# Gate and up tiles of a SwiGLU layer: three products into 256 columns in place of two into 512 and 256, and no sums of halves

## The reference, cut to what matters

```python
    ffn = (jax.nn.silu(h @ w_ffn_gate[l]) * (h @ w_ffn_up[l])) @ w_ffn_down[l]
    h = layer_norm(DEEPNORM_ALPHA * h + ffn, ln2_g[l], ln2_b[l])
```

## Time and profile before

| | |
|---|---|
| median of 3 runs | 1360.66 us |
| lowest and highest | 1360.02 and 1361.16 us |
| the profiled execution, from its first to its last instruction (span) | 1358.1 us |
| TensorE matmuls busy | 1348.0 us, 99% |
| TensorE weight loads busy | 1213.2 us, 89% |
| VectorE busy | 890.4 us, 66% |
| ScalarE busy | 651.7 us, 48% |
| mean granted TensorE clock | 0.999 of full speed |

### The profile page before, as it was taken

The page is one execution under the profiler, slowest core; times in us unless marked ns, Lnnn a source line. Parts: engine busy times, 40 slices in busy tenths (PEclk is TensorE's granted clock), DMA queues, the critical chain, the costliest instruction groups (busy, mean ns, idle before and its releaser), DMA issues.

```text
span 1358.1 us, 25677 instructions
## 1 busy us (share of the span) xinstructions
PE 1348.0 (99%) x9644; PEld 1213.2 (89%) x9644; DVE 890.4 (66%) x1320; ACT 651.7 (48%) x910; POOL 23.0 (2%) x50
## 2 busy tenths in 40 slices
PE   9999999999999999999999999999999999999998
PEld 8999999999999998878888888888888888888897
DVE  6787868677785766578666666666666655545545
ACT  5556556474656444355444444444444453334332
POOL 0022000000000000000000000000000000000000
PEclk9999999999999999999999999999999999999999
DMA  8656544445465776644656555555555665556563
GB/s 282 202 190 182 163 150 155 156 145 167 141 183 184 242 228 199 230 173 136 195 184 196 186 187 192 191 187 190 191 189 186 208 231 192 189 171 201 170 204 106
DMA packets 79773, 253.19 MB, mean 186 GB/s; under 512 B 16544, under 2 KB 17504, under 8 KB 79584
## 3 DMA queue, kind: packets, MB, share of 16 engines
q1 hardware_dynamic: 78304, 251.69, 56.5%
q0 software_dynamic: 1408, 0.63, 0.2%
HBM read 248.08 MB, written 2.10 MB: 184 GB/s over the span
## 4 chain that ended last, share of the span: by engine, by line
PE 98%; DVE 1%; ACT 1%; DMA 0%; issue 0%; SPq 0%; DVEq 0%
PE ps L890 23%; PE ps L893 12%; PE ps L879 11%; PE ps L880 10%; PE ps L881 10%; PE ps L902 9%; PE ps L904 9%; PE ps L903 9%; PE ps L1098 1%; PE ps L1117 1%; PE ps L1094 1%; DMA xrow<-x 0%; PE ps L1029 0%; PE ps L1070 0%; PE ps L1043 0%; PE ps L1051 0%
## 5 line engine op out<-in xcount | busy, mean ns | idle before, releaser
L464 DVE TENSOR_TENSOR wlo<-raw,whi 128x1024 fp32r<-128x1024 f32 x450 | 546.6, 1223 | 287.1 <-ACT whi L508 286.0
L508 ACT ACTIVATE whi<-raw 128x1024 fp32r<-128x1024 f32 x450 | 475.1, 1057 | 406.6 <-PE ps L904 184.8
L890 PE MATMUL ps<-hT,whi 128*128 128x512 f32 x1376 | 477.1, 390 | 0.0
L893 PE MATMUL ps<-hT,wlo 128*128 128x256 f32 x1376 | 388.0, 282 | 0.0
L890 PEld LDWEIGHTS ps<-hT,whi 128*128 128x128 f32 x1376 | 258.3, 188 | 54.1
L893 PEld LDWEIGHTS ps<-hT,wlo 128*128 128x128 f32 x1376 | 260.1, 189 | 0.0
L879 PE MATMUL ps<-xT,whi 128*128 128x256 f32 x784 | 224.1, 286 | 0.6 <-DVE wlo L464 0.6
L880 PE MATMUL ps<-xT,whi 128*128 128x256 f32 x784 | 219.0, 279 | 0.0
L881 PE MATMUL ps<-xT,wlo 128*128 128x256 f32 x784 | 218.6, 279 | 0.0
L879 PEld LDWEIGHTS ps<-xT,whi 128*128 128x128 f32 x784 | 147.4, 188 | 1.9 <-issue 1.1
L880 PEld LDWEIGHTS ps<-xT,whi 128*128 128x128 f32 x784 | 147.5, 188 | 0.2
(11 more groups left out here) (271 smaller groups left out, 1407.0 us busy)
## 6 DMA issues: line engine op xcount, KB each, us to landing
raw<-slabs SPq DMA_DIRECT2D x450, 512.0 KB, 3.8
xrow<-x SPq DMA_DIRECT2D x4, 512.0 KB, 6.8
rows<-x SPq DMA_DIRECT2D x4, 512.0 KB, 6.7
gb<-ln_rows SPq DMA_DIRECT2D x4, 512.0 KB, 7.9
eraw<-slabs SPq DMA_DIRECT2D x4, 512.0 KB, 7.0
gb<-ln_rows SPq DMA_DIRECT2D x1, 2048.0 KB, 8.3
out<-rows SPq DMA_DIRECT2D x8, 256.0 KB, 2.4
yb<-u SPq DMA_DIRECT2D x32, 24.0 KB, 3.1
```

The costliest lines, as they stand in the source:

```text
L464: unit.tensor_tensor(wlo[:, s, :], raw[:, s, :], whi[:, s, :].bitcast(F32), ALU.subtract).then_inc(done, 1 + empty_after)
L508: nc.scalar.activation(whi[:, s, :], raw[:, s, :], ACT.Copy).then_inc(hi_ready, 1 + empty + first)
L890: mm(ps[:, bank, :], hi, src[:, kt].rearrange("p a t -> p (a t)"), start=(first and n == 0), stop=False)
L893: ins = mm(ps[:, bank, TOK:512], lo, src[:, kt, 0, :], start=False, stop=done)
```

## The change

The gate and up tiles are made by `fold_tile`, and `feature_tile` goes. The sums of halves (L1872, 88 of them) go, with `tmp[0]` and `tmp[2]`: the Silu reads bank 0 (bank 4 in the second pair) itself, and the product reads bank 1 (bank 5) itself. What frees a bank is now the Silu for the gate's and the product for the up's (`ffn_silu`, `ffn_prod`), so these two semaphores take the place of `row_free` in this stage, and the counts of `row_free` behind it become smaller by 88. VectorE makes its third low part before it waits for the up tile, and its fourth after the product and not before it. All buffers stay at their addresses.

```diff
@@ ScalarE
-                    ac.wait_ge(row_free, i * 4 + 11 + 2 * e)
-                    nc.scalar.activation(tmp[:, 1, :], tmp[:, 0, :], ACT.Silu).then_inc(ffn_silu, 1)
+                    if first and e == 0:
+                        ac.wait_ge(early_used, 1)
+                    else:
+                        ac.wait_ge(slab_used, i * FFN_PER + (FFN0 + 4 * e + 2))
+                    nc.scalar.activation(tmp[:, 1, :], ps[:, 4 if first and e == 1 else 0, 0:TOK], ACT.Silu).then_inc(ffn_silu, 1)
...
@@ TensorE
-            def feature_tile(bank, s, b, src, kts, first, last, whi=whi, wlo=wlo):
-
-                for n, kt in enumerate(kts):
-                    hi = whi[:, s, (b + n) * P:(b + n + 1) * P]
-                    lo = wlo[:, s, (b + n) * P:(b + n + 1) * P]
-                    mm(ps[:, bank, :], hi, src[:, kt].rearrange("p a t -> p (a t)"),
-                       start=(first and n == 0), stop=False)
-                    done = last and n == len(kts) - 1
-                    ins = mm(ps[:, bank, TOK:512], lo, src[:, kt, 0, :], start=False, stop=done)
-                return ins
...
-            def panel(src, src_ready, n_slabs, slot0, v, low, m):
+            def panel(src, src_ready, n_slabs, slot0, v, low, m, read=()):
...
                     if k == 0:
                         row_bank(m + t)
+                        if read:
+                            pe.wait_ge(read[t], FT)
...
-                    ins = feature_tile(e, 2 * e + h, n, hT, (k,), k == 0, k == KT - 1, ehi, elo)
+                    ins = fold_tile(e, 2 * e + h, n, hT, (k,), k == 0, k == KT - 1, ehi, elo)
...
                     if not bank:
-                        row_bank(i * 4 + (8 + e))
+                        pe.wait_ge((ffn_silu, ffn_prod)[e % 2], i * 2 + e // 2)
                     for h in range(2):
                         k = 2 * e + h
                         late_low(i * FFN_PER + (FFN0 + k))
-                        feature_tile(bank + e % 2, k % RING, 0, hT, range(8 * h, 8 * h + 8), h == 0, h == 1
-                                     ).then_inc(slab_used, 1)
+                        fold_tile(bank + e % 2, k % RING, 0, hT, range(8 * h, 8 * h + 8), h == 0, h == 1
+                                  ).then_inc(slab_used, 1)
...
@@ VectorE
-                    lows(0, 1)
-                    tile_sum(tmp[:, 0, :], 0, v + 1)
-                    lows(2)
-                    tile_sum(tmp[:, 2, :], 1, v + 3)
+                    lows(0, 1, 2)
+                    if first and e == 0:
+                        ve.wait_ge(early_used, 2)
+                    else:
+                        ve.wait_ge(slab_used, v + 4)
+                    ve.wait_ge(ffn_silu, n + 1)
+                    V.tensor_tensor(tmp[:, 3, :], tmp[:, 1, :], ps[:, 5 if first and e == 1 else 1, 0:TOK], ALU.mult
+                                    ).then_inc(ffn_prod, 1)
                     lows(3)
-                    ve.wait_ge(row_free, i * 4 + (12 + 2 * e))
-                    ve.wait_ge(ffn_silu, n + 1)
-                    V.tensor_tensor(tmp[:, 3, :], tmp[:, 1, :], tmp[:, 2, :], ALU.mult).then_inc(ffn_prod, 1)
```

More of the change, by code:

```diff
@@ L872, in row_bank, with fold_tile @@
                 pe.wait_ge(row_free, m + 1)
-            def fold_tile(bank, s, b, src, kts, first, last):
+            def fold_tile(bank, s, b, src, kts, first, last, whi=whi, wlo=wlo):
                 for n, kt in enumerate(kts):
@@ L1273, in _ @@
                     panel(act, act_lo, DOWN_PER, DOWN_PER * p, i * (2 * DOWN_PER) + DOWN0 + DOWN_PER * p, late_low,
-                          i * 4 + (8 + 2 * FT + 2 * p))
-            panel(act, act_lo, DOWN_PER, 2 * DOWN_PER, DOWN0 + 2 * DOWN_PER, late_low, 8 + 2 * FT + 4)
-            v, m = DOWN0 + 3 * DOWN_PER, 8 + 2 * FT + 6
+                          i * 4 + (8 + 2 * p), (ffn_silu, ffn_prod) if p == 0 else ())
+            panel(act, act_lo, DOWN_PER, 2 * DOWN_PER, DOWN0 + 2 * DOWN_PER, late_low, 8 + 4)
+            v, m = DOWN0 + 3 * DOWN_PER, 8 + 6
             def last_part(k, t):
@@ L1321, in _ @@
             offset(0, 2, 3, True)
-            pe.wait_ge(row_free, 2 + 8 + 2 * FT + 7)
+            pe.wait_ge(row_free, 2 + 8 + 7)
             turn_shift(1, 0)
@@ L1863, in ffn_turn @@
             def ffn_turn(i, first):
[L1864 to L1873, removed]
                 for e in range(2):
@@ L1920, in down_residual @@
             def down_residual(n, t, to=None):
-                residual(n, t, n * 2 + (8 + 2 * FT), n + 6 * HG + 4, n * DOWN_PER + DOWN0 + DOWN_PER - 1, to)
+                residual(n, t, n * 2 + 8, n + 6 * HG + 4, n * DOWN_PER + DOWN0 + DOWN_PER - 1, to)
             def times_gain(n, t):
```

## The result

The changed kernel takes 1368.13 us, the median of four runs (1365.34 to 1370.95), against 1360.38 us for the kernel before (1360.02 to 1361.16) on the same chip. The ratio is 1.0057, 95% interval 1.004 to 1.0074: slower, by some 8 us. The forecast was 1365.4 with a range of 1364.0 to 1371.0.

The account below looks back on a forecast made before the run. TensorE's gapless stream of products bounds the kernel, at 346.7 ns a block in the gate and up stage. 1408 blocks at 350.0 ns add 4.7 us to 1360.66, giving 1365.4 us; range 1364.0 to 1371.0.

Parts of the forecast that it names:

- The price per block: Gate and up stage: three products instead of two cost 3.3 or 6.7 ns more per block, 4.7 or 9.4 us over 1408.
- The choice between the two paces: Gate and up stage: 350.0 ns per block taken (+4.7 us, chance 0.53), with 353.3 ns (+9.4 us) as upper bound.
- The likeness: Head-stage products behind transposes ran at the faster pace; the gate and up stage also begins behind transposes, so 350.0 ns.
- The case I called the rival: Gate and up stage at the slower pace, 353.3 ns a block as in GLU: 1370.1 us, chance 0.34 with mixtures.
- The other side: VectorE, ScalarE and the banks: removing 60 us of sums buys nothing, and new waits on Silu and product cost nothing.
- the larger loop body: PE's loop grows from 64 x 2 to 64 x 3 products and loads; rival of exposed instruction fetches, about 1385 us, chance 0.02.
- The rival "faster": Gate and up products of 256 columns pack closer, under 115.6 ns each; at 0.11 us throughout, 1337.2 us; chance 0.03.
- Weight loads: Gate and up stage: PEld, busy 88.67 of 100 us, loses its slack as in GLU; no cost added beyond the pace.
- 118 ns each at the least: GLU stage: length of a weight load, read from 731 loads filling 86.00 us.
- that rival: Weight loads can't run beside products, so the third adds its whole length per block: 166 us, 1526 us; chance under 0.01.

Follow-up runs that it names:

- experiment 2: The kernel before with only the 512-column product split into two of 256, sums and waits unchanged: 1370.03 us, ratio 1.0064.
- experiment 3: The changed kernel with feature_tile's two products (512 and 256 columns) put back, new readers and waits kept: 1361.24 us, ratio 1.0006.
- experiment 4: The changed kernel with three identity transposes into free bank 7 between the unrolled tiles and the loop: 1366.08 us.
- experiment 7: The kernel before with the 512-column product split into 256, 128 and 128 columns, four products a block: 1510.84 us, ratio 1.1105.
- experiment 1: The changed kernel run again with no edit: six runs from 1365.47 to 1371.02 us, ratio 1.0057 to the kernel before.
- experiment 5: The changed kernel with two plain float32 products into free bank 7 between the unrolled tiles and the loop: 1366.53 to 1366.79 us.
- experiment 6: The kernel before with three identity transposes into bank 6 ahead of the GLU stage: 1360.02 us, ratio 0.9996.

## Why the prediction was right, and where its reason was not

**The price per block** held: 3.3 or 6.7 ns, times 1408, and the runs lie at 1365.3 to 1366.2 and 1370.0 to 1371.0 where 1365.4 and 1370.1 were worked out. That the price is the third product's, and not the readers' or the waits', is shown by experiments 2 and 3. It is the price at this place of `hT`: moved by 64 to 192 bytes, three products took 355.0 to 360.0 ns.

**The choice between the two paces** is the step that failed: "By that likeness I take 350.0 ns". In the head stage transposes had led to the faster pace in 12 of 12 places, but the transposes of L1225 don't fix it: over ten runs the changed kernel took it four times, and in experiment 4 the stage starts behind the same transposes at 281 ns throughout. The likeness itself was read rightly and holds further than I knew: in all fourteen traces the stretches behind the transposes of the probabilities have the faster pace, 168 of 168. But of the five traces that begin the gate and up stage with three products and an unmoved `hT`, only one starts it fast. How these transposes differ from the others stays open. I had one profile, in which each place has one pace, and took it for a rule; that a pace could differ from run to run of the same program wasn't visible there. The case I called the rival came in six of ten runs. The 1365.4 of the forecast came only in the other four, by chance and not by the likeness. The range held because it had room for both paces: the median of 1368.13 is only the middle between two runs of either kind, and no run had that time.

**The other side**, hidden at no cost, came out: no wait of PE in the stage; the Silu with 4.2 us to spare against 4 worked out; VectorE at 57 us of 100 against near 55; no gap at the down projection. In 660 to 1100 us the changed kernel's trace has no packet on either instruction queue (one in the earlier trace rows), so the larger loop body cost nothing.

**The rival "faster"** needed under 115.6 ns a product. No run of three products had it, at five places of the operand.

**Weight loads.** The prediction found the loads at the edge (busy 100%) and added nothing for it. The busy share says less than it seems: a load is shown with 188 to 192 ns, and in experiment 7 one follows the other after 113.3. So "118 ns each at the least" was wrong, and the sum of that rival, made with 113.3, would be 1520 and not 1526 us. Three such loads are an estimated 340 of the 350 ns. The low chance of that rival stands on the traces: matmuls and weight loads are both busy in all of the same 86.00 us, where three loads and their products take 353.3 ns a block, and the third load, with its product, lengthened a block by 3.3 or 6.7 ns and not by 113. Whether the two paces come from this edge stays open: no shift gave three products less than 350.0 ns, which fits a bound by the loads, but the pair, with loads busy 87%, took 353.3 ns too once `hT` was moved.

## What to carry to other kernels

Where TensorE ran without a gap, removing 60 us of work from the reader of its banks was worth nothing, and each product more was paid: 3.3 or 6.7 ns for the third in a block, 100 ns or more for the fourth. Count the weight loads beside the columns: in this kernel a load of 128 float32 columns took 113 ns, and two products of 128 columns in place of one of 256 made the block as long as its four loads. A stream that is repeated a thousand times deserves its pace read to 0.1 ns from the first and last start; at this size, the place of an operand or an interruption ahead of the loop decided as much as the number of products, and single runs fell into two groups. So take several runs before a difference of 5 us in 1365 is believed, and don't take the pace of one profile for a rule.

## What the runs showed of the hardware that was not expected

- One and the same stream of products of 256 columns has two paces, 350.0 and 353.3 ns per three, at full clock and with TensorE busy throughout. It keeps the one that it started with for up to 98 us (GLU and the gates ahead of it) or 486 us (experiment 1), and changed at an interruption by other matmuls in experiments 4, 5 and 6.
- At the start of the gate and up stage the pace differs between runs of one program: four of ten runs had the faster, and one of six in experiment 2. At five places of the head stage, too, the pace differs between traces of the same code.
- Moving the streamed operand by 64 to 192 bytes gave 355.0 to 360.0 ns with three products, and 353.3 in place of 346.7 with two, where every second block paid about 15 ns.
- Weight loads in a row took 113.3 ns each (experiment 7), though each is shown with 188 to 192 ns.
